# Chunk inverses of a delta rule: five levels on 32 by 32 blocks, the sixth by its corner, widened to 64 for the last

## The reference, cut to what matters

```python
diff = gc[..., :, None] - gc[..., None, :]
decay = jnp.where(incl, jnp.exp(jnp.where(incl, diff, 0.0)), 0.0)
kb = kc * bc[..., None]
a_mat = jnp.where(strict, jnp.einsum('nbhik,nbhjk->nbhij', kb, kc) * decay, 0.0)
t_mat = lax.linalg.triangular_solve(a_mat, eye, left_side=True, lower=True, unit_diagonal=True)
u = jnp.einsum('nbhij,nbhjv->nbhiv', t_mat, vc * bc[..., None])
w = jnp.einsum('nbhij,nbhjk->nbhik', t_mat, kb * jnp.exp(gc)[..., None])
```

## Time and profile before

| | us |
|---|---|
| median of 3 runs (2898.32 to 2900.61) | 2898.88 |
| the profiled execution, its own time | 2902.46 |
| its span | 2900.6 |
| the stage: line 1794's first product, next stage's first product | 355.79, 489.12 |

### The profile page before, as it was taken

How to read it: one execution, slowest core, us unless ns; L and a number is a source line. 1 busy time by engine, 2 the same in 40 slices (tenths; PEclk the granted TensorE clock), 3 DMA queues, 4 the chain that set the end, 5 groups by cost and what they waited for, 6 DMA issues and landing times.

```text
span 2900.6 us, 43152 instructions
## 1 busy us (share of the span) xinstructions
PE 2806.2 (97%) x17446; PEld 2355.7 (81%) x17446; DVE 1564.3 (54%) x2638; ACT 1151.3 (40%) x1911; POOL 226.1 (8%) x251
## 2 busy tenths in 40 slices
PE   7998999999999999999999999999999999999998
PEld 4866898788888888788888888888888788888887
DVE  6745575555444436765644337644436775544346
ACT  4335553342422324565422225523224574332234
POOL 0001174200000000201000000000000101000001
PEclk9999999999999999999999999999999999999998
DMA  6222000122223232351223332232332341322321
GB/s 246 70 82 79 8 4 3 54 92 98 80 99 99 98 104 101 103 134 48 88 95 95 102 109 87 73 101 95 99 105 99 106 110 52 107 97 95 102 94 59
DMA packets 78262, 258.99 MB, mean 89 GB/s; under 512 B 10161, under 2 KB 12337, under 8 KB 77425
## 3 DMA queue, kind: packets, MB, share of 16 engines
q1 hardware_dynamic: 78064, 256.24, 27.4%
HBM read 234.70 MB, written 3.15 MB: 82 GB/s over the span
## 4 chain that ended last, share of the span: by engine, by line
PE 65%; DVE 6%; ACT 2%; issue 1%; POOL 0%; DVEq 0%; ACTq 0%; POOLq 0%
PE pair L249 20%; PE pair L251 20%; PE pair L250 20%; PE pair L2889 2%; DVE work_at L346 1%; PE pair L2856 1%; DVE w_lo_at L192 1%; PE pair L2899 1%; DVE residual L352 1%; DVE h_lo_at L357 1%; DVE rstd_at L544 1%; ACT w_hi_at L184 1%; PE pair L405 0%; PE pair L2859 0%; DVE scores_at L3163 0%
## 5 line engine op out<-in xcount | busy, mean ns | idle before, releaser
L249 PE MATMUL pair<-h_hi_at,w_hi_at 128*128 128x512 f32 (+1 forms) x2112 | 781.2, 370 | 17.3 <-DVE h_lo_at L357 12.9
L250 PE MATMUL pair<-h_lo_at,w_hi_at 128*128 128x512 f32 (+1 forms) x2112 | 768.8, 364 | 0.0
L251 PE MATMUL pair<-h_hi_at,w_lo_at 128*128 128x512 f32 (+1 forms) x2112 | 768.7, 364 | 0.0
L184 ACT ACTIVATE w_hi_at<-w_raw 128x1024 fp32r<-128x1024 f32 x340 | 358.8, 1057 | 886.3 <-PE pair L251 864.5
L192 DVE TENSOR_TENSOR w_lo_at<-w_raw,w_hi_at 128x1024 fp32r<-128x1024 f32 x340 | 430.1, 1265 | 311.5 <-ACT w_hi_at L184 311.3
L249 PEld LDWEIGHTS pair<-h_hi_at,w_hi_at 128*128 128x128 f32 x2112 | 399.3, 189 | 97.7 <-DVE h_lo_at L357 20.6
L250 PEld LDWEIGHTS pair<-h_lo_at,w_hi_at 128*128 128x128 f32 x2112 | 399.9, 189 | 62.9 <-issue 0.5
L251 PEld LDWEIGHTS pair<-h_hi_at,w_lo_at 128*128 128x128 f32 x2112 | 399.7, 189 | 62.9
L2575 DVE TENSOR_TENSOR work_at<-pair,rstd_at 128x512 f32<-128x512 f32 x176 | 121.2, 691 | 350.4 <-PE pair L251 350.2
L249 PE MATMUL pair<-a_hi_at,w_hi_at 128*128 128x512 f32 (+1 forms) x792 | 290.1, 366 | 0.0
L251 PE MATMUL pair<-a_hi_at,w_lo_at 128*128 128x512 f32 (+1 forms) x792 | 289.4, 365 | 0.0
(11 more groups left out here) (461 smaller groups left out, 3958.3 us busy)
## 6 DMA issues: line engine op xcount, KB each, us to landing
w_raw<-in_weights SPq DMA_DIRECT2D x431, 512.0 KB, 3.5
k_stack_at<-stack_hi_at SPq DMA_DIRECT2D x32, 128.0 KB, 2.3
k_stack_at<-stack_lo_at SPq DMA_DIRECT2D x32, 128.0 KB, 2.3
residual<-in_x SPq DMA_DIRECT2D x1, 2048.0 KB, 11.4
cos_sin_at<-rope_table SPq DMA_DIRECT2D x2, 1024.0 KB, 4.8
by_sin_at<-delta_at SPq DMA_DIRECT2D x32, 64.0 KB, 2.0
by_sin_at<-kd_at SPq DMA_DIRECT2D x32, 64.0 KB, 2.1
q_stack_at<-stack_hi_at SPq DMA_DIRECT2D x16, 128.0 KB, 2.3
```

The lines of the kernel that those rows point to most:

```text
L184: eng.activation(self.w_hi[:, g % self.split].rearrange("p k n -> p (k n)"), self.w_raw[:, slot], ACT.Copy).then_inc(self.w_hi_ready, 1)
L249: pe.matmul(out, sh, mh, start=start, stop=False)
L250: pe.matmul(out, sh, ml, start=False, stop=False)
L251: return pe.matmul(out, sl, mh, start=False, stop=stop)
```

## The change

The levels 0 to 4 (l < SMALL = 5) work on the four 32 by 32 blocks of the diagonal: for each head four products of 32 rows and 32 columns, on four different parts of the array. The tiles a, b, u, t and the PSUM results are half as wide (4 x 32 = 128 elements per row). Level 5 joins pairs of 32-blocks by their corner alone, as level 6 did and does for the 64-blocks: a_mid holds that part of A, `corners` issues two products per head. POOL's new `widen` puts u and t on the diagonal of 64-wide tiles (times a mask own_half, the other half zero), four operations of 256 elements per chunk; DVE then writes the negated corners into them from PSUM, eight operations of 32 rows by 128 elements, in place of four of 128 rows by 256. `strengths` writes per direction four diagonal blocks, two middle corners and the far corner (seven operations) where it wrote three; POOL's `weigh_far` weighs a_mid too. Two copies for each direction set up beta_mid once. `levels` in DRAM keeps its size.

```diff
-    H, STEPS = 64, LEVELS - 1
+    H, Q, STEPS, SMALL = 64, 32, LEVELS - 1, LEVELS - 2
...
+        mid_pairs = (((1, 0), (3, 2)), ((0, 1), (2, 3)))
...
                 def blocks(out, stationary, moving):
-                    for hs in small_slices:
-                        for rows in (upper, under):
+                    for hs in quarter_slices:
+                        for rows in quarters:
                             last = pe.matmul(out[rows, hs], stationary[rows, hs], moving(rows, hs), start=True, stop=True)
+                    return last
+
+                def corners(out, pairs, stationary, moving):
+                    for hs in quarter_slices:
+                        for rows_in, rows_out in pairs:
+                            into, of = quarters[rows_out], quarters[rows_in]
+                            last = pe.matmul(out[into, hs], stationary[of, hs], moving[of, hs], start=True, stop=True)
                     return last
...
                             elif l < STEPS:
                                 pe.wait_ge(u_ready[d], STEPS * c + l)
-                                last = blocks(bank[4 + d], b, lambda rows, hs: u[rows, d, hs])
+                                pe.wait_ge(far_ready, c + 1)
+                                last = corners(bank[4 + d], mid_pairs[d], a_mid[:, c % 2], u[:, d])
...
+                            elif l < STEPS:
+                                stay = [(out, out) for _, out in mid_pairs[d]]
+                                back = [(out, into) for into, out in mid_pairs[d]]
+                                corners(bank[6 + d], stay, t[:, d], x_mat[:, d]).then_inc(u_summed[d], 1)
+                                corners(bank[2 + d], back, x_mat[:, d], t[:, d]).then_inc(t_summed[d], 1)
...
-                    for rows, columns in ((upper, upper), (under, under)):
-                        dve.tensor_tensor(heads(a_mat[:, c % 2, d])[rows], raw[rows, :, columns], faded[rows, :, columns], ALU.mult)
+                    for rows in quarters:
+                        dve.tensor_tensor(heads(a_mat[:, c % 2, d])[rows], raw[rows, :, rows], faded[rows, :, rows], ALU.mult)
+                    for into, out in mid_pairs[d]:
+                        rows, columns = quarters[into], quarters[out]
+                        dve.tensor_tensor(heads(a_mid[:, c % 2])[rows], raw[rows, :, columns], faded[rows, :, columns], ALU.mult)
...
+                            if l == SMALL:
+                                dve.wait_ge(u_summed[d], STEPS * c + l)
+                                dve.wait_ge(widened, 4 * c + 2 * d + 1)
+                                for into, out in mid_pairs[d]:
+                                    last = dve.tensor_scalar(in_half(u_wide[:, c % 2, d], out)[:, :, half_columns(into)],
+                                                             in_half(bank[6 + d][:, 0:4 * Q], out), -1.0, None, ALU.mult)
+                                last.then_inc(u_ready[d], 1)
+                                dve.wait_ge(t_summed[d], (STEPS - 1) * c + l)
+                                dve.wait_ge(widened, 4 * c + 2 * d + 2)
+                                for into, out in mid_pairs[d]:
+                                    last = dve.tensor_scalar(in_half(t_wide[:, d], into)[:, :, half_columns(out)],
+                                                             in_half(bank[2 + d][:, 0:4 * Q], into), -1.0, None, ALU.mult)
+                                last.then_inc(t_ready[d], 1)
...
+                def widen(c):
+                    for d in DIRECTIONS:
+                        for src, dst, ready in ((u_mat[:, d], u_wide[:, c % 2, d], u_ready[d]),
+                                                (t_mat[:, d], t_wide[:, d], t_ready[d])):
+                            pool.wait_ge(ready, STEPS * c + SMALL)
+                            if c >= 2:
+                                pool.wait_ge(placed[d], c - 1)
+                            pool.tensor_tensor(dst.rearrange("p (h e n) -> p h e n", h=HEADS, e=2),
+                                               heads(src)[:, :, None, :].to_broadcast([P, HEADS, 2, Q]),
+                                               own_half.rearrange("p (e n) -> p e n", e=2)[:, None, :, :].to_broadcast(
+                                                   [P, HEADS, 2, Q]), ALU.mult).then_inc(widened, 1)
...
                 def weigh_far(c):
+                    mid = heads(a_mid[:, c % 2])
+                    pool.tensor_tensor(mid, mid, column(beta_mid[:, c], Q), ALU.mult)
...
+                    widen(c)
                     if c + 1 < NCH:
                         weigh(c + 1)
                         weigh_far(c + 1)
```

More of the change, by code:

```diff
@@ L1718, in delta_inverse @@
         low, near, x_mat = sb("low", [P, 2, 512]), sb("near", [P, 2, 512]), sb("x", [P, 2, 4 * H])
-        a_mat, a_far, b_mat = sb("a", [P, 2, 2, 4 * H]), sb("a_far", [P, 2, 4 * H]), sb("b", [P, 2, 2, 4 * H])
-        u_mat, t_mat, beta_far = sb("u", [P, 2, 2, 4 * H]), sb("t", [P, 2, 2, 4 * H]), sb("beta_far", [P, NCH, HEADS])
+        a_mat, a_mid, a_far = sb("a", [P, 2, 2, 4 * Q]), sb("a_mid", [P, 2, 4 * Q]), sb("a_far", [P, 2, 4 * H])
+        b_mat, u_mat, t_mat = sb("b", [P, 2, 2, 4 * Q]), sb("u", [P, 2, 4 * Q]), sb("t", [P, 2, 4 * Q])
+        u_wide, t_wide = sb("u_wide", [P, 2, 2, 4 * H]), sb("t_wide", [P, 2, 4 * H])
+        beta_mid, beta_far = sb("beta_mid", [P, NCH, HEADS]), sb("beta_far", [P, NCH, HEADS])
         heads = lambda x: x.rearrange("p (h n) -> p h n", h=HEADS)
@@ L1725, in delta_inverse @@
         small_slices = [slice(h * H, (h + 1) * H) for h in range(HEADS)]
+        quarter_slices = [slice(h * Q, (h + 1) * Q) for h in range(HEADS)]
+        quarters = [slice(r * Q, (r + 1) * Q) for r in range(4)]
         ident = kit.square("ident")
-        small_ident = levels[:, 0, STEPS]
+        small_ident, own_half = levels[:, 0, STEPS, 0:Q], levels[:, 0, SMALL]
         upper, under = slice(0, H), slice(H, P)
         far_in, far_out = (under, upper), (upper, under)
+        mid_pairs = (((1, 0), (3, 2)), ((0, 1), (2, 3)))
+        in_half = lambda x, r: heads(x)[quarters[r]]
+        half_columns = lambda r: slice(r % 2 * Q, (r % 2 + 1) * Q)
         DIRECTIONS = range(2)
@@ L1800, in _ @@
                 for c in range(NCH):
-                    u, t = u_mat[:, c % 2], t_mat[:, c % 2]
+                    u, t, u_all = u_mat, t_mat, u_wide[:, c % 2]
                     for l in range(LEVELS):
                         for d in DIRECTIONS:
-                            if l < STEPS:
-                                pe.wait_ge(b_ready[d], STEPS * c + l + 1)
-                                b = b_mat[:, d, (STEPS * c + l) % 2]
+                            if l < SMALL:
+                                pe.wait_ge(b_ready[d], SMALL * c + l + 1)
+                                b = b_mat[:, d, (SMALL * c + l) % 2]
                             if l == 0:
@@ L1837, in _ @@
                                 for hs in small_slices:
-                                    last = pe.matmul(bank[6 + d][rows, hs], t[rows, d, hs], x_mat[rows, d, hs], start=True,
+                                    last = pe.matmul(bank[6 + d][rows, hs], t_wide[rows, d, hs], x_mat[rows, d, hs], start=True,
                                                      stop=True)
@@ L1878, in _ @@
                 for d in DIRECTIONS:
-                    dve.tensor_copy(beta_far[far_in[d]], beta[far_in[d], d]).then_inc(far_beta, 1)
+                    for into, _ in mid_pairs[d]:
+                        dve.tensor_copy(beta_mid[quarters[into]], beta[quarters[into], d])
+                    dve.tensor_copy(beta_far[far_in[d]], beta[far_in[d], d])
                 for l in (1, 2, 4, 5):
@@ L1958, in _ @@
                                 act.wait_ge(u_summed[d], STEPS * c)
-                            rows = slice(0, P) if l < STEPS else far_out[d]
-                            act.activation(x_mat[rows, d], bank[4 + d][rows, 0:4 * H], ACT.Copy).then_inc(x_ready[d], 1)
+                            rows, width = (slice(0, P), 4 * Q) if l < STEPS else (far_out[d], 4 * H)
+                            act.activation(x_mat[rows, d, 0:width], bank[4 + d][rows, 0:width], ACT.Copy).then_inc(x_ready[d], 1)
                         prepare(c + 1, l)
@@ L1965, in _ @@
                         for rows in (upper, under):
-                            act.activation(whole[rows, :, rows], heads(u_mat[:, c % 2, d])[rows], ACT.Copy)
+                            act.activation(whole[rows, :, rows], heads(u_wide[:, c % 2, d])[rows], ACT.Copy)
                     for d in DIRECTIONS:
@@ L3708, in shape_constants @@
         levels.append((i // (2 * s) == j // (2 * s)) & (i // s % 2 == 1) & (j // s % 2 == 0))
-    in_blocks = lambda m: np.concatenate([m[:HD, :HD], m[HD:, HD:]])
-    levels = np.stack([np.stack([in_blocks(m) for m in (*order, i == j)], axis=1)
```

(3 more changed lines are left out.)

38 lines of the change are left out of this document (19 added, 19 removed).

## The result

The changed kernel takes 2969.96 us (median of 4 runs, 2967.68 to 2971.09), the one before 2899.12 on the same chip: a ratio of 1.0237, 95% interval 1.0224 to 1.025. Forecast were 2887 and a range up to 2914. It is 71 us slower, and both the sign and the range were wrong. The profiled execution took 2971.09 for a span of 2969.3.

A forecast was written before the change was run, and what follows sets the result against it. TensorE, busy 97% of the span, was taken to bound the kernel, locally the chunk-inverse stage. Start +1.2, chunk 0 -1.5, chunks 1 to 4 -9.2, chunk 5 -5.2, clock +3: -11.7 us, giving 2887, range 2878 to 2914.

The forecast's parts named there:

- The bound, the place, one for one: Stage of the chunk inverses, 133.3 us: TensorE is the bound, and what shortens the stage shortens the program one for one.
- the +1.2: Before chunk 0: first DVE burst 1.7 us longer, weighting and b 0.6 shorter, taken as +1.2 us.
- g = 0.26: A level's group of products on TensorE: 8 rounds of four at 0.0325 us, 0.26 us where it was 0.465.
- Rival 1: Instruction supply paces TensorE's groups: g still 0.465, +13 us, 2912; at g = 0.56, 2925; chance 0.23.
- rival 3: Each TensorE instruction keeps its mean step of 29 ns, narrow costing as much as wide: g = 0.93, 2980; chance 0.05.
- The chunk's end: From level 4's start to the chunk's end: 10.8 us against 9.33, 1.5 longer, the new wait being DVE's 4.2 us burst.
- Clock, +3: Chunk ends: TensorE's idling may bring 1.2 GHz stretches after some, from nothing to 5 x 1.7 us, taken as +3.
- Chunk 5, -5.2: Last chunk, nothing prepared: levels of 1.9 us against 3.04, level 0 in 0.9 instead of 1.4, together -5.2 us.

The follow-up runs named there:

- the burst: Kernel before, with 256 products of 64 by 64, then 512 of 32 by 32, behind the next stage's idle products, no waits: 32-wide part 26.5 us, one execution of 2951.02.

## Why the prediction was wrong, step by step

- **The bound, the place, one for one: right.** Of the 68.7 us between the two spans 65.8 are in this stage, 2.7 ahead of it and 0.2 behind. The 2.7 can't be read as the +1.2 that was forecast there: the stage's start differs by 4.8 us among kernels that are the same up to it.
- **g = 0.26: right for the array, wrong as the beat.** This is the step that failed: "I take 0.26 because that dense stretch is itself paced by 59 ns rounds and so is no limit of the supply". That stretch has 41 instructions, fewer than the store of some 500, so it says nothing of the supply in either direction, and I read it as a proof that there is room. At 3.8 us a block, the 384 instructions of a level's six groups alone take 5.7 us, where 2.5 were forecast for all of it. A chunk of some 2010 instructions has a floor of 7.9 x 3.8 = 30 us. The 20 more blocks could have been counted beforehand: the page of before has 139 blocks on its instruction queue.
- **Rival 1 named the mechanism and mis-sized it.** It took 0.465 to 0.56 as the slowest group, 2912 to 2925. The supply's 15 ns make 64 instructions 0.95 us, and that is the g of rival 3 (0.93, 2980, with a chance of 0.05). That the time came out near rival 3's is luck of the numbers: its price, 29 ns for each product with its load, was near; its reason, a fixed cost of a product whatever its width, was wrong: in the burst, instructions in store start 4.5 ns apart.
- **The Trainium skill's** page TensorEngine Tiling (Array Packing), section Instruction Overhead, was set aside as holding per tile. Its advice, not to take a tiling from a dimension that is small already, was right here, for the reason of the supply. By its 60 cycles a product would cost an estimated 25 ns at 2.4 GHz, and the burst's rows show no such price on the queue: out of store a MATMUL with its load starts every 9 ns. The 60 cycles can still hold on one tile, since four tiles share the burst and each starts a MATMUL every 36 ns on average.
- **The chunk's end: right in its parts, and too short.** Burst forecast 4.2 us, measured 383.69 to 388.1, 4.4; then eight copies of 0.29; the far product waits for u_wide. POOL's widening 0.72 for an estimate of 0.74, b 1.69 for four, so 0.42 each, as estimated. From the burst's end to the next chunk it is 4.5 us (388.1 to 392.58) where 3.45 were forecast, as the far products ran at half clock (0.50 in 390.5 to 392.6). TensorE's idle time ahead of the far product is 1.3 to 1.6 us, not 3, because its stops had moved its own work to later. DVE timeline of chunk 0's end, changed kernel:

```profile
383.69 1.18 DVE L1883 TENSOR_TENSOR inv_a<-pair,inv_near 32x128 f32<-32x128 f32 x4
384.89 0.59 DVE L1886 TENSOR_TENSOR inv_a_mid<-pair,inv_near 32x128 f32<-32x128 f32 x2
...
387.75 0.42 DVE L1888 TENSOR_TENSOR inv_a_far<-pair,inv_near 64x256 f32<-64x256 f32 x1
388.09 0.57 DVE L1931 TENSOR_SCALAR inv_u_wide<-pair 32x128 f32<-32x128 f32 x2
```

- **Clock, +3: mis-sized.** I looked for it at chunk ends; the changed kernel has 0.58 over the whole stage. It isn't the stops alone: with all products split, TensorE stops just as much and has 0.97 over its stage. It goes with the narrow products: 0.66 with half of them and few stops, 0.50 in the burst. But each of these has idle time too, and between stops a block of 32 by 32 products gives the array less work than a block of split ones (a group start every 0.28 us against 0.47), so the tile's size by itself is not shown to be the cause. At 0.50 groups start 0.43 apart instead of 0.28.
- **Chunk 5, -5.2: the largest gain of any one chunk became a loss.** It takes 31.9 us (525.68 to 557.56) where 20.9 stood, because a loop of short waits still has to have its instructions: six stops in it make 10.7 us.

What stays open is how much of the changed kernel's 33.4 us a chunk the clock has by itself. The kernel with split products has 10% more instructions, full clock and the same chunk, so the low clock and the longer end together may hold what those instructions would have cost; an estimate from 193 instructions at 15 ns is up to 3 us a chunk. No run kept the clock up with the narrow tiles.

## What to carry to other kernels

Count the instructions of a stretch, not only its columns, and hold them against its time: on this chip TensorE was given 256 per about 3.8 us, 15 ns each, once its store of some 500 was used up, and a quiet stretch is not saved up beyond that. An fp32 product costs four (two loads, two products), so tiles cut in half in both directions halve the work of the array and double what the supply has to bring. And where an engine's burst is just hidden, a saving elsewhere uncovers it: move the burst first, then save.

## What the runs showed of the hardware that was not expected

- 256 instructions every 3.73 to 4.00 us on TensorE in the burst, and blocks 3.4 to 4.7 us apart for products of 32 by 32, at either clock, and of 64 by 32, with the engine at work again 1.2 to 1.5 us after a block's packet has landed. In the kernel before the blocks of this stage came 3.3 us apart at the least and 4.8 on the mean.
- Some 528 instructions start at 4.5 ns each out of store before the first stop.
- With narrow products (32 by 32, four side by side) the granted clock was at 0.50 for most of a stage (0.58 on the mean) in which split ones of 64 by 32, with as many stops, had 0.97.
